# Hybrid convolution / MLP trunk on one core: when returned blocks, sigmoid tables and a bias are taken

## The reference

```
layer 0: u = rmsnorm(h);  a = u @ w_pw1 + b_pw1           (2048 -> 4096)
         v = val * sigmoid(gate);  v = causal depthwise conv (31 taps) + b_dw
         h = h + silu(rmsnorm(v)) @ w_pw2 + b_pw2
layer 1: B, C, v = split(rmsnorm(h) @ w_in)               (2048 -> 6144)
         h = h + (B * causal depthwise conv (3 taps) of (C * v)) @ w_out
both:    h = h + square(relu(rmsnorm(h) @ w1)) @ w2       (hidden 8192)
         h = h + sigmoid(rmsnorm(h) @ w_gate) * (p @ w_proj)
out    = rmsnorm(h)
```

## Time and profile before

| what | us |
|---|---|
| median of 3 runs | 2313.45 (2311.26 to 2314.07) |
| the profiled execution | 2314.72 |
| its span in the trace | 2312.9 |
| TensorE matmul busy | 2271.6 (98%) |
| VectorE busy | 1437.8 (62%) |
| ScalarE busy | 1022.9 (44%) |
| GpSimd busy | 1.6 (0%) |

### The profile page before, as it was taken

How to read it: one execution, slowest core, us unless ns; L and a number is a source line. 1 busy time by engine, 2 the same in 40 slices (tenths; PEclk the granted TensorE clock), 3 DMA queues, 4 the chain that set the end, 5 groups by cost and what they waited for, 6 DMA issues and landing times.

```text
span 2312.9 us, 28592 instructions
## 1 busy us (share of the span) xinstructions
PE 2271.6 (98%) x9970; PEld 1872.4 (81%) x9970; DVE 1437.8 (62%) x1715; ACT 1022.9 (44%) x1186; POOL 1.6 (0%) x9
## 2 busy tenths in 40 slices
PE   8999999999999999999999999999999999999997
PEld 7888677888888888888778888888888888888886
DVE  6999865654654654666566666665555555555665
ACT  1000545534534544555554344554345345445555
POOL 0000000000000000000000000000000000000000
PEclk9999999999999999999999999999999999999999
DMA  9444267765765765777667777777667667667772
GB/s 340 148 146 146 87 209 220 238 227 183 243 227 181 243 226 180 246 239 220 212 219 234 235 226 215 230 252 233 209 207 229 214 205 229 218 199 233 261 235 107
DMA packets 493946, 494.51 MB, mean 214 GB/s; under 512 B 257920, under 2 KB 296000, under 8 KB 493120
## 3 DMA queue, kind: packets, MB, share of 16 engines
q1 hardware_dynamic: 492336, 491.83, 66.8%
q10 hardware_dynamic: 1408, 0.89, 0.1%
q0 software_dynamic: 144, 1.05, 0.1%
HBM read 460.16 MB, written 33.55 MB: 213 GB/s over the span
## 4 chain that ended last, share of the span: by engine, by line
PE 75%; issue 14%; DVE 4%; DMA 4%; ACT 1%; SPq 1%; DVEq 0%; ACTq 0%; POOL 0%; POOLq 0%
PE acc L409 25%; PE acc L411 25%; PE acc L410 25%; DMA staged<-prows 2%; DMA pT<-staged 2%; DVE prows L897 1%; SPq L307 1%; DVE wlo L831 1%; DVE res L887 0%; DVE work L882 0%; ACT work L584 0%; ACT b_hi L604 0%; DVE res L870 0%; PE acc L530 0%; PE acc L532 0%
## 5 line engine op out<-in xcount | busy, mean ns | idle before, releaser
L831 DVE TENSOR_TENSOR wlo<-raw,whi 128x1024 fp32r<-128x1024 f32 x732 | 871.2, 1220 | 399.0 <-ACT whi L551 392.4
L551 ACT ACTIVATE whi<-raw 128x1024 fp32r<-128x1024 f32 x732 | 752.9, 1054 | 619.4 <-PE acc L411 616.1
L409 PE MATMUL acc<-whi,b_hi 128*128 128x512 f32 x1632 | 637.3, 391 | 6.9 <-DVE wlo L831 3.4
L411 PE MATMUL acc<-whi,b_lo 128*128 128x512 f32 x1632 | 635.1, 389 | 0.0
L410 PE MATMUL acc<-wlo,b_hi 128*128 128x512 f32 x1632 | 635.0, 389 | 0.0
L409 PE MATMUL acc<-whi,a_hi 128*128 128x512 f32 x1280 | 500.9, 391 | 11.5 <-DVE wlo L831 8.1
L411 PE MATMUL acc<-whi,a_lo 128*128 128x512 f32 x1280 | 499.3, 390 | 0.0
L410 PE MATMUL acc<-wlo,a_hi 128*128 128x512 f32 x1280 | 499.2, 390 | 0.0
L409 PEld LDWEIGHTS acc<-whi,b_hi 128*128 128x128 f32 x1632 | 306.3, 188 | 76.4 <-DVE wlo L831 5.1
L411 PEld LDWEIGHTS acc<-whi,b_lo 128*128 128x128 f32 x1632 | 306.3, 188 | 64.0
L410 PEld LDWEIGHTS acc<-wlo,b_hi 128*128 128x128 f32 x1632 | 306.4, 188 | 63.4 <-issue 0.2
(11 more groups left out here) (134 smaller groups left out, 602.6 us busy)
## 6 DMA issues: line engine op xcount, KB each, us to landing
raw<-in_mlp_w SPq DMA_DIRECT2D x256, 1024.0 KB, 5.6
raw<-in_sc_w_in SPq DMA_DIRECT2D x48, 1024.0 KB, 5.6
raw<-in_cf_w_pw SPq DMA_DIRECT2D x64, 512.0 KB, 9.2
raw<-in_ple_w_gate SPq DMA_DIRECT2D x32, 1024.0 KB, 5.7
staged<-prows SPq DMA_DIRECT2D x240, 128.0 KB, 3.3
pT<-staged SPq DMA_DIRECT2D x56, 512.0 KB, 3.3
raw<-in_cf_w_pw SPq DMA_DIRECT2D x16, 1024.0 KB, 5.3
raw<-in_sc_w_out SPq DMA_DIRECT2D x16, 1024.0 KB, 6.1
```

Of the source, the lines that this page charges most:

```text
L409: nc.tensor.matmul(o, xhi[:, k, s], hi, start=first and c == 0, stop=False)
L411: mm = nc.tensor.matmul(o, xlo[:, k, s], hi, start=False, stop=last and c == 1)
L551: nc.scalar.activation(whi[:, e % SLOTS, :, :], raw[:, e // 2, 2 * (e % 2):2 * (e % 2) + 2, :], ACT.Copy).then_inc(hi_ready, 1)
L831: nc.vector.tensor_tensor(wlo[:, e % SLOTS, :, :], raw[:, e // 2, 2 * (e % 2):2 * (e % 2) + 2, :], whi[:, e % SLOTS, :, :].bitcast(F32), A ...
```

## The change

- `operand_hi` and `operand_lo` of a returned block are taken behind split 7 in place of ahead of it; the new norm and its square root stand between splits 6 and 7. Where a gain is multiplied in, ScalarE counts each of four chunks up, and VectorE takes chunk by chunk.
- Hidden results: relu and square of the first token half, then of the second. VectorE turns the first half when it is squared, then the second (`turn_hidden`).
- Gate results: a sigmoid of one column into `table` stands ahead of the waits.
- The bias of pw2: GpSimd loads it into a part of `emb` when 8 chunks of the projection are done, and adds it to `h` in four additions. VectorE's bias addition goes. ScalarE waits for the four ahead of the fifth embedding copy, which overwrites the bias's place.
- The last gate: the gated add stands behind split 3 in place of ahead of it. The last block's splits come in the order 0, 1, 2, 4, 5, 6, 7, 3, and the result of the block before behind them; TensorE waits ahead of half 3 for all eight.

```diff
-    RES = dict(T=1, x=1, o=1, t=1, xh=1, s=1)
+    RES = dict(T=1, x=1, o=1, t=1, xh=4, s=1)
-        bias2 = work[:, :, :].rearrange("p c n -> p (c n)")
+        bias2 = emb[:, 1, 1, :]
 # TensorE, last block
-                pe.wait_ge(lo_ready, HALVES * (g1.b + BLOCKS - 1) + e + 1)
+                pe.wait_ge(lo_ready, HALVES * (g1.b + BLOCKS - 1) + (e + 1 if e < SLOTS - 1 else HALVES))
 # ScalarE, hidden result
+                    act.wait_ge(tr_ready, r.T)
                     for m in range(2):
-                        last = nc.scalar.activation(zb[:, m:m + 1, :], acc[:, bass.ds(2 * r.pair + m, 1), :],
+                        relu = nc.scalar.activation(zb[:, m:m + 1, :], acc[:, bass.ds(2 * r.pair + m, 1), :],
                                                     ACT.Relu, scale=rinv[:, m:m + 1])
-                    last.then_inc(acc_free, 1)
-                    act.wait_ge(acc_free, r.a + 1)
-                    act.wait_ge(tr_ready, r.T)
-                    nc.scalar.activation(res[:, :, :], zb, ACT.Square).then_inc(res_ready, 1)
+                        relu.then_inc(relu_ready, 1)
+                        act.wait_ge(relu_ready, 2 * r.hd + m + 1)
+                        if m:
+                            nc.scalar.sem_inc(acc_free, 1)
+                        nc.scalar.activation(res[:, m, :], zb[:, m, :], ACT.Square).then_inc((sq_half, res_ready)[m], 1)
                 if r.kind in ("gate", "gate_last"):
+                    first = 2 if r.kind == "gate" else 2 + BLOCKS
+                    nc.scalar.activation(table[:, bass.ds(r.j + first, 1)], ident[:, 0:1], ACT.Sigmoid)
                     act.wait_ge(half_used, HALVES * r.b + HALVES)
 # ScalarE, order of a block (VectorE's run alike)
                 for e in range(HALVES):
                     if e == 3 and before:
                         before()
-                    if e == at and after:
-                        after()
                     split_hi(b, e)
                     if between:
                         between(e)
+                if after:
+                    after()
+                def between(e):
+                    if e == 6 and new_norm is not None:
+                        take_root(new_norm)
 # ScalarE, embedding copies
             take_root(NORM_CONV, *rb_parts)
+            act.wait_ge(biased, BLOCKS)
             embedding_out(4)
 # ScalarE, last block
-            for e in range(SLOTS):
-                if e == 3:
-                    process(r)
+            for e in range(SLOTS - 1):
                 split_hi(r.b + 1, e)
             for e in range(SLOTS, HALVES):
                 late_split_hi(r.b + 1, e)
-                if e == 4:
-                    keep(r)
+            split_hi(r.b + 1, SLOTS - 1)
+            process(r)
+            keep(r)
 # VectorE
-                if r.kind == "pw2":
-                    nc.vector.tensor_tensor(res[:, :, :], res[:, :, :],
-                                            bias2[:, cols(r.j)].unsqueeze(1).to_broadcast([P, 2, NB]),
-                                            ALU.add).then_inc(res_ready, 1)
-                else:
-                    nc.vector.sem_inc(res_ready, 1)
+                nc.vector.sem_inc(res_ready, 1)
+            def turn_hidden(r):
+                dve.wait_ge(staged_ready, 64 * r.T)
+                dve.wait_ge(sq_half, r.hd + 1)
+                nc.vector.transpose(out=turned_blocks[:, :, 0:4, :], in_=res_blocks[:, :, 0:4, :])
+                dve.wait_ge(res_ready, r.t + 1)
+                nc.vector.transpose(out=turned_blocks[:, :, 4:8, :], in_=res_blocks[:, :, 4:8, :]).then_inc(tr_ready, 1)
                     for c in range(4):
+                        dve.wait_ge(xhi_ready, xh + c + 1)
                         last = nc.vector.scalar_tensor_tensor(
-            dve.wait_ge(bias2_ready, 16)
+            dve.wait_ge(biased, BLOCKS)
 # GpSimd
-            pool.wait_ge(y_ready, UNITS)
+            pool.wait_ge(val_done, UNITS)
             nc.gpsimd.dma_start(bias2, t_in["cf_b_pw2"][0].partition_broadcast(P)).then_inc(bias2_ready, 16)
+            pool.wait_ge(bias2_ready, 16)
+            for j in range(BLOCKS):
+                nc.gpsimd.tensor_tensor(h[:, :, cols(j)], h[:, :, cols(j)],
+                                        bias2[:, cols(j)].unsqueeze(1).to_broadcast([P, 2, NB]),
+                                        ALU.add).then_inc(biased, 1)
```

More of the change, by code:

```diff
@@ L939, in run @@
                         before()
-                    if e == 7 and after:
-                        after()
                     split_lo(b, e)
@@ L1168, in _ @@
             run(win.b + 1, lambda: gate_c((win.b, win.a)))
[L1169 removed]
+            run(win.b + 2, lambda: c_times_v(0), lambda: short_taps(0))
             with dve.Fori(1, BLOCKS) as j:
```

76 lines of the change are left out of this document (40 added, 36 removed).

## The result

| | median us (runs) | profiled execution | span | first to last matmul of the 92 blocks |
|---|---|---|---|---|
| before | 2313.19 (4) | 2314.72 | 2312.9 | 2035.05, from 267.83 |
| after | 2295.99 (4) | 2294.58 | 2292.8 | 2008.88, from 273.85 |

The changed kernel is faster: ratio 0.9920, 95% interval 0.9908 to 0.9933. The forecast was 2293.9, in a range of 2286 to 2303; for the profiled execution it was 2295.1.

A forecast was written before the change was run, and what follows sets the result against it. TensorE was taken as the bound, with 33.1 us of excess over its block pace. Terms of 26.0 us won less 6.4 lost gave 19.6 net: median 2293.9 us, profiled execution 2295.1, range 2286 to 2303.

The forecast's parts named there:

- pw2 stretch: Four pw2 blocks and first MLP block: all waits go, from bias, bias add and returned-block order; 9.8 of 9.98 us won.
- 32 MLP blocks: MLP blocks behind the first: hidden results taken in halves return sooner, 1.3 of 2.27 us won.
- gate stretch: Later gate blocks and first win block: half-7 wait and slow clock go, half-3 partly; 10.8 of 13.76 us won.
- last block: The very last block: a 1.5 us wait at half 3 replaces 2.92 at half 4; 1.55 us won.
- GpSimd's adds: Beside the convolution taps: four adds hold VectorE 2.24 us each, 2.6 absorbed; 6.4 us lost.
- (c): In the pw2 stretch: returned block no longer ahead of split 7, so ready at 15.2, ahead of 16.3 in first MLP block.
- 1 + 1 + 0.8: Gate stretch, waits left: about 1 us at half 3 of two blocks, 0.8 from a late returned block behind the loop.
- Taps with gaps of that length: Profile sign at the convolution taps: gaps as long as the GpSimd adds, 2 to 3 us.
- no slow clock before the end: Profile sign for TensorE: the granted clock doesn't fall to its lower level until the end.
- rival without disturbance: At the taps: GpSimd's adds and VectorE don't disturb one another, 26.0 us won, 2287.5 us; chance 0.32.
- the one with the returned blocks passed on to half 0: Gate blocks: returned block delays next block's first splits, 1.8 us in three blocks; 14.2 us won; chance 0.18, GpSimd case included.
- The far end: GpSimd adds at 4.5 us each, VectorE loses 15.4 us, 10.6 won; chance 0.18, shared with gate waits kept elsewhere.

The follow-up runs named there:

- e3: Changed kernel with returned blocks and the new norm ahead of split 7 again, as before; 2300.08 us in one run.
- e2: Kernel before with only the bias moved to GpSimd and VectorE's bias addition gone; 2312.97 us, ratio 1.0001.
- e11: Changed kernel with the order of returned blocks, the sigmoid ahead of the waits and the chunks undone together; 2307.61 us in one run.
- e6: Changed kernel with the loop's three gate blocks written out, so no table load stands at the loop's top; 2293.89 us in one run.
- e10: Changed kernel with VectorE waiting for all four high parts of a returned block again, chunks undone; 2299.38 us in one run.
- e4: Changed kernel without the one-column sigmoid ahead of the waits; 2297.53 us in one run.
- e7: Changed kernel with hidden results processed whole again: two relus, one square, one transpose; 2301.14 us in one run.
- e8: Changed kernel with early GpSimd adds, gate loop written out, last block's split 3 sooner, w_out's first returned block ahead of split 7; 2285.36 us, ratio 0.9882.
- e9: Changed kernel with one GpSimd add in the middle of the tap row of each of chunks 9 to 12; 2295.88 us, ratio 0.9927.
- e1: Changed kernel with two GpSimd adds at the start of chunk 9's taps and two at chunk 10's; 2296.38 us, ratio 0.9929.

## Why the prediction held, and where it did not

| term | predicted | measured |
|---|---|---|
| pw2 stretch | 9.8 | 9.4 |
| 32 MLP blocks | 1.3 | 2.0 |
| gate stretch | 10.8 | 10.5 |
| 48 blocks | 1.8 | 1.9 |
| two blocks | 0.7 | 0.8 |
| last block | 1.55 | 1.57 |
| won behind the first pw2 matmul | 26.0 | 26.2 |
| GpSimd's adds | -6.4 | -6.0 |
| net, profiled pair | 19.6 | 20.1 |

**The ledger.** Cutting the trace at block boundaries against a pace of 21.76 us, and asking of each excess which wait makes it, gave every stretch to within 0.7 us. The forecast of the profiled execution, 2295.1, is 0.5 above the measured one.

**The pw2 stretch** came out in sum, but the prediction's three reasons aren't three parts. It had the third (c), the order, as needed for the first MLP block; e3 has the old order and no wait there, e2 has the old order and chunks and is long there by 0.5 only. The late returned block of before was mostly the delay by the bias passed on. With the order, table and chunks undone and the bias kept, 1.83 us are left (e11), 1.23 of them in the first MLP block. The 0.60 that remain in the kernel after lie in the first pw2 block, and no run takes them away.

**The gate stretch** is right in size and in what is left: 1.06, 1.04 and 1.13 us against "1 + 1 + 0.8"; the mechanism for the first two is shown by e6, whose unrolled loop takes them away, and the size of the chunks at the third by e10 (2.22 without them). The order alone would not have done it: e3, e4, e10 and e11 show that order, table and chunks share the gain, each at a half of its own and together at half 7. Of the drain that the Trainium skill (ScalarE: Activation LUTs, What ACT_TABLE_LOAD costs) adds to each load nothing is seen: in the kernel after the operation behind the load at 1124.62 starts at 1125.91, 1.29 later, and the load itself starts when the splits ahead of it end (1121.65 + 2.96).

**Hidden results** won more than forecast in this pair (2.0 against 1.3 in the 32 blocks); e2, with the old hidden results, against the other traces gives 1.1 to 1.5. The prediction reckoned 0.6 us for a block that returns just in time; e7 shows about 1.0 at the two late ones (1.34 against 0.28 in the MLP of layer 0, 1.26 against 0.31 at the first of layer 1; against the latest of the other traces with hidden halves and the new order, 0.67 and 0.59, still 0.7) and smaller ones in others. So 0.6 was somewhat small; which of the step's parts (relu, square, transpose) was mis-sized no run tells.

**The last block** came as worked out: split 3 was forecast to end at 2283.4 - 2277.88 = 5.5 us into the block, and does at 5.54; the wait is 1.5. That two late parts ahead of it do no harm, which e8 uses, follows from the same sum.

**The GpSimd adds.** The size, 6.4, is near the 6.0, but it is put together otherwise, and that the two meet is partly luck: three misses cancel. The prediction let each add stop VectorE for 2.24 us, 9.0 in all, and subtracted 2.6 of idle time, 6.4. Measured: 7.8 us on VectorE; less what it has in hand, 4.45 at the sum; and the slow clock behind the longer wait adds 1.5 that the prediction had left out ("no slow clock before the end"). From chunk 8's product at 145.91 to the last at 243.3 VectorE's chunk takes (97.4 - 3.6) / 7 = 13.40, TensorE's before took 13.81: 0.41 x 8 = 3.3 in hand, and 7.8 - 3.3 = 4.5. "Taps with gaps of that length" was wrong: a held instruction shows up as a longer one, with no gap; and of the four in the changed kernel only two were taps, the first two of a row. "Four adds of 2 to 3 us" held for three; the first took 7.44, kept out by the row that was running. The rival without disturbance (2287.5) and the one with the returned blocks passed on to half 0 are both excluded: four instructions were held, and no wait at half 0 is there. The far end (15.4 us) is as well, since the sum matmul is late by 4.45 and not by 12.

**Still open.** The one place that became worse is w_out's first block, 0.83 against 0.36 before. In the kernel after the new order has a part in it: VectorE's product of the short convolution (L1175), whose low part TensorE waits for, starts straight behind split 7, with no idle time. In e3, where it stands ahead of split 7, it waits for its transfer and is earlier in the block (12.65 us behind the block's start instead of 13.31), and that block is long by 0.15 only. First the kernel after, then e3:

```profile
1421.67 1.23 DVE L836 TENSOR_TENSOR wlo<-raw,whi 128x1024 fp32r<-128x1024 f32 x1 [1.44 <-ACT whi L552]
1422.82 1.22 DVE L1175 TENSOR_TENSOR work<-pT,work 128x1024 f32<-128x1024 f32 x1
```

```profile
1427.96 1.23 DVE L1175 TENSOR_TENSOR work<-pT,work 128x1024 f32<-128x1024 f32 x1 [1.91 <-DMA pT<-staged]
```

The old order is not enough, though: e11 has it and is at 0.81, e8 has it in this block and is at 0.84. There the product waits for its transfer as in e3, but the transpose that sends it stands later in the block (2.18 and 2.49 us instead of 1.83), behind taps that had waited longer for their input from DRAM. In e9, with the code of the kernel after, the transpose stands at 3.19 and the block is long by 1.59. What moves the transfer wasn't tried.

## What to carry to other kernels

Cut the trace of an engine that is the bound at its own block boundaries, and hold every stretch against its free pace: the excesses add up to what can be won, and each has a wait with a name. That GpSimd is idle doesn't hide work moved to it: it cost VectorE 1.1 to 2.15 us for each add of 128 x 1024 in SBUF that met it at work on operands in SBUF, in all places that were tried, so it belongs where VectorE waits (here 6.0 us between two places of the same four adds). When several parts mend one wait, undo them together as well as one by one: parts that cost 3.6, 1.5 and 0.8 us alone cost 9.8 together, 1.7 of it by the clock.

## What was unexpected in the hardware

- The middle of an unbroken row of VectorE taps, a start every 0.395 us, kept a GpSimd add out altogether: the first add of the kernel after and the four of e9 waited 5.3 to 6.3 us, to the row's end. Adds that followed one another took 2.4 to 2.5 us each, and the VectorE instruction that started beside one took 2.45 to 2.57 instead of 0.42 to 0.48. VectorE's additions, its scalar_tensor_tensor taps (e1) and its operations with one tensor operand (L1045: 1.93 instead of 0.41, L1047: 2.43 instead of 0.35) were all held.
- A wait of 4.0 us on TensorE (with one of 1.75 us at 243.85, ahead of it) was followed by a granted clock of 0.50, 1.2 GHz; the wait of 1.49 at the same place wasn't. The lower level lasted 3.41 us in the kernel after, e1, e3, e6 and e9, and 6.83 in e2, e4, e7, e10 and e11, which is one reason why their starts are not alike. The length of a wait alone does not tell whether the clock falls: it fell behind waits of 2.00 and 2.26 us in the kernel before and 2.08 in e11, and did not behind 2.92 in the last block of the kernel before or 3.10 at 246.69 in e1.
